# Attention inside a one-core diffusion step: a third bank for scores, the row sums of a tile in one stretch, and GpSimd's second addition without its wait for the split

## What is computed

```
def _block_attention(q, k, v):          # q (B,Lq,H,D), k/v (B,Lk,KVH,D)
    ...
    def one(qblk):                      # blocks of 128 queries
        s = jnp.einsum('bqkgd,bskd->bkgqs', qblk, k).astype(jnp.float32) * scale
        p = jax.nn.softmax(s, axis=-1).astype(v.dtype)
        return jnp.einsum('bkgqs,bskd->bqkgd', p, v)
...
aq = _rmsnorm(aq.reshape(B, L, AT_HEADS, AT_HD), p['q_norm_g'])
keys = jnp.concatenate([_apply_rope(ak, cos, sin), cache['k'].astype(ak.dtype)], axis=1)
vals = jnp.concatenate([av, cache['v'].astype(av.dtype)], axis=1)
y_at = _block_attention(_apply_rope(aq, cos, sin), keys, vals)
```

## Time and profile before

| | |
|---|---|
| median of three runs | 2370.05 us |
| profiled execution, its own time | 2371.3 us |
| its span, first to last instruction | 2369.5 us |
| TensorE matmuls busy in the span | 2280.0 us, 96% |
| VectorE / ScalarE / GpSimd busy | 1390.6 / 805.7 / 336.2 us |
| granted TensorE clock, mean | 0.988 |
| the eight tiles | about 1163.5 to 1391.9 us of the span |

### The profile page before, as it was taken

One profiled execution on the slowest core, in us unless ns is written; L12 is line 12 of the kernel. 1 busy time (PEld: TensorE's weight loads), 2 busy tenths in 40 slices (PEclk: granted clock), 3 DMA queues, 4 the chain that ended last, 5 costly groups with the idle time before them and its releaser, 6 DMA issues. The chain is left out here.

```text
span 2369.5 us, 42943 instructions
## 1 busy us (share of the span) xinstructions
PE 2280.0 (96%) x17607; PEld 2025.9 (85%) x17607; DVE 1390.6 (59%) x2116; ACT 805.7 (34%) x1398; POOL 336.2 (14%) x291
## 2 busy tenths in 40 slices
PE   6999999999999899998899989998999999999997
PEld 5887779999999889998755569877999999998886
DVE  4331266533555466665555446768676676677877
ACT  5321132213333233223344444325323223234444
POOL 0000000001110011111377631000111111120001
PEclk9999999999999999999999989999999999999999
DMA  6325632235452532224101038421222222259434
GB/s 279 121 85 182 225 112 104 104 127 210 155 170 88 199 107 76 89 71 158 44 19 68 36 120 309 153 89 59 79 105 91 79 105 91 74 181 273 130 97 124
DMA packets 126875, 295.55 MB, mean 125 GB/s; under 512 B 19809, under 2 KB 63281, under 8 KB 117377
## 3 DMA queue, kind: packets, MB, share of 16 engines
q1 hardware_dynamic: 98112, 238.67, 29.9%
q10 hardware_dynamic: 24640, 39.46, 4.5%
q0 software_dynamic: 3968, 15.21, 1.7%
HBM read 207.83 MB, written 85.53 MB: 124 GB/s over the span
## 5 line engine op out<-in xcount | busy, mean ns | idle before, releaser
L62 PE MATMUL ps<-prj_w,h_hi 128*128 128x512 f32 (+1 forms) x864 | 255.1, 379 | 4.5 <-DVE h_lo L755 4.5
L62 PE MATMUL ps<-h_hi,fill_whi 128*128 128x384 f32 x672 | 235.4, 350 | 4.9 <-ACT fill_st L1119 2.4
L62 PE MATMUL ps<-h_lo,fill_whi 128*128 128x384 f32 x672 | 226.3, 337 | 3.8 <-issue 3.8
L62 PE MATMUL ps<-wt 128*128 128x320 f32 (+2 forms) x1046 | 227.2, 327 | 2.3 <-DVE merged L3341 1.3
L62 PE MATMUL ps<-h_hi,fill_wlo 128*128 128x384 f32 x672 | 226.4, 337 | 0.2 <-issue 0.2
L62 PE MATMUL ps<-ys,mergedr 128*128 128x256 f32 (+1 forms) x1056 | 219.3, 296 | 0.4 <-issue 0.4
L62 PE MATMUL ps<-zb,mergedr 128*128 128x320 f32 (+2 forms) x764 | 200.4, 327 | 4.9 <-issue 2.7
L62 PE MATMUL ps<-zb,wt 128*128 128x384 f32 (+3 forms) x758 | 200.2, 325 | 0.0
L62 PEld LDWEIGHTS ps<-prj_w,h_hi 128*128 128x128 f32 x864 | 158.1, 191 | 43.1 <-issue 10.6
L62 PEld LDWEIGHTS ps<-wt 128*128 128x128 f32 x1046 | 179.6, 189 | 16.7 <-issue 2.6
L62 PEld LDWEIGHTS ps<-ys,mergedr 128*128 128x128 f32 x1056 | 174.2, 190 | 0.7 <-issue 0.7
(11 more groups left out here) (508 smaller groups left out, 4694.9 us busy)
## 6 DMA issues: line engine op xcount, KB each, us to landing
wraw<-in_w_ffn_in SPq DMA_DIRECT2D x22, 1024.0 KB, 5.2
prj_raw<-in_w_ada SPq DMA_DIRECT2D x16, 1024.0 KB, 5.9
fill_raw<-in_w_fill SPq DMA_DIRECT2D x30, 512.0 KB, 4.6
wtf<-a_dram SPq DMA_DIRECT2D x55, 256.0 KB, 2.6
bg_dram<-fill_st ACTq DMA_DIRECT2D x72, 192.0 KB, 2.0
xf<-bg_dram POOLq DMA_DIRECT2D x24, 576.0 KB, 7.5
tok_dram<-prj_tst ACTq DMA_DIRECT2D x45, 256.0 KB, 2.1
prj_raw<-in_w_tok SPq DMA_DIRECT2D x10, 1024.0 KB, 7.1
```

The costliest lines, as they stand in the source:

```text
L62: mm = pe.matmul(out, lhs[a], rhs[b], start=first and n == 0, stop=last and n == 2, skip_group_check=onto)
```

## The change

- **Third score bank.** `ST` now means banks 4, 5 and 6; score u = 18i + m goes to bank 4 + u mod 3 and waits for the exponential three scores before. The row sums leave bank 6 for bank 3.
- **Row sums in one stretch.** The sums of tile i-1 are computed in tile i, all three trios at once, behind head 2. Trio buffers that hold sums get four slots (two of them over the staging buffers of `branch`); the others stay two and two. `shifts` of the next tile, which uses bank 3 as well, waits for the reciprocal.
- **Score halves between maxima.** The scores are issued by m: 4, 3, 4, 3 and 4 of them between heads, instead of 4, 4, 4, 2 and 4. ScalarE's copies of queries and shifts stand at m = 4 and 11.
- **GpSimd.** The wait of the second additions for the split is removed.
- **Edges.** The query transposes of tile 1 move ahead of the last half product of `branch`. ScalarE makes three of the six copies for the next phase in tile 6 and three in tile 7; VectorE makes the subtractions one by one, the last behind the last normalization.

```diff
-    RING, TRIO = 6, 3
+    TRIO, SLOTS = 3, 4
...
-            pt = [over(f"pt{i}", [P, KV, G * P]) for i in range(RING)]
+            pt = [over(f"pt{i}", [P, KV, G * P]) for i in range(4)]
+            trio = [over(f"trio{i}", [P, KV, G * P]) for i in range(2)]
...
+        def held(n):
+
+            b, r = divmod(n, TRIO)
+            return trio[b % SLOTS] if r == TRIO - 1 else pt[b % 2 * 2 + r]
+
...
                 gp.wait_ge(sem["paired"], 2 * n + 1)
-                if split is not None and split[0] <= LAST:
-                    gp.wait_ge(sem["part"], 2 * split[0] + split[1] + 1)
                 gp.tensor_tensor(c[:], c[:], b[:], ALU.add).then_inc(sem["paired"], 1)
...
             def shifts(i, kv):
                 pe.wait_ge(sem["mx"], AH * i + G * kv + G)
                 pe.wait_ge(sem["pte"], turn(i, 2 + kv))
+                if kv == 0 and i >= 2:
+                    pe.wait_ge(sem["rc"], i - 1)
...
-                if u >= 2:
-                    pe.wait_ge(sem["ex"], u - 1)
+                if u >= 3:
+                    pe.wait_ge(sem["ex"], u - 2)
+                if u == 2:
+                    pe.wait_ge(sem["b0ev"], 24)
...
-                out, at = ps[:, ST + kv, :], slice(j * P, j * P + P)
+                out, at = ps[:, ST + u % 3, :], slice(j * P, j * P + P)
...
+            def sums(i):
+
+                pe.wait_ge(sem["pte"], (turn(i + 2, 1) if i + 2 <= LAST else turn(LAST, 3)) + 1)
+                if i == LAST:
+                    pe.wait_ge(sem["norm"], i)
+                for g in range(NT // TRIO):
+                    n = NT // TRIO * i + g
+                    if n < LASTG:
+                        pe.wait_ge(sem["paired"], 2 * n + 2)
+                        mm = add(held(TRIO * n + TRIO - 1), g == 0, g == 2)
+                    else:
+                        for x in range(TRIO):
+                            mm = add(held(TRIO * n + x), False, x == TRIO - 1)
                 mm.then_inc(sem["sums"], 1)
...
                 shifts(i, 1)
                 head(0)
-                step(0)
-                step(1)
+                steps(0, 4)
                 head(1)
                 if more:
                     queries(i + 1, 1)
-                step(2)
-                step(3)
+                steps(4, 7)
                 head(2)
                 if i:
-                    sums(3 * i - 1)
+                    sums(i - 1)
                 values(i, 0)
                 head(3)
-                step(4)
-                step(5)
+                steps(7, 11)
                 head(4)
                 if more:
                     shifts(i + 1, 0)
-                step(6)
+                steps(11, 14)
                 head(5)
                 if i:
                     spread_sums(i - 1)
                 values(i, 1)
-                sums(3 * i)
                 head(6)
-                step(7)
-                step(8)
+                steps(14, 18)
                 head(7)
                 if i + 2 <= LAST:
                     queries(i + 2, 0)
                 values(i, 2)
-                sums(3 * i + 1)
...
                 shift_scores(0, 2 * u - 39)
+                if u == 23:
+                    queries(1, 0)
                 branch(range(u, u + 1), (2, 4))
-            queries(1, 0)
...
-                for j in range(NT):
-                    exponentials(i, j)
-                    if more and j == 1:
+                for m in range(2 * NT):
+                    if more and m == 4:
                         queries(i + 1, 1)
-                    if more and j == 5:
+                    if more and m == 11:
                         shifts(i + 1, 0)
-                    if not more and j < 6:
-                        ahead(j)
+                    exponentials(i, m // KV, m % KV)
+                    if i >= LAST - 1 and m in (7, 13, 17):
+                        ahead(3 * (i - LAST + 1) + (7, 13, 17).index(m))
...
+                    if i == LAST and h in (0, 1, 2):
+                        ahead(h)
                     if i >= 1 and h == 2:
                         inverted(i - 1)
-                    if i == LAST and h == 5:
-                        ahead()
+                    if i == LAST and h == 3:
+                        ahead(3)
...
+            ahead(4)
             inverted(LAST)
             normed(LAST)
+            ahead(5)
```

More of the change, by code:

```diff
@@ L1925, in attention @@
         STAGES = 6
+        with ExitStack() as later:
+            trio += [later.enter_context(nc.sbuf_tensor(f"att_trio{i}", [P, KV, G * P], F32)) for i in range(2, SLOTS)]
         b0st = [ph.sb(f"b0st{i}", [P, TH]) for i in range(STAGES)]
@@ L1930, in attention @@
         block = ph.block()
-        PT, ST, SB, OB = 3, 4, 6, 7
+        PT, ST, OB = 3, 4, 7
+        def held(n):
+            b, r = divmod(n, TRIO)
+            return trio[b % SLOTS] if r == TRIO - 1 else pt[b % 2 * 2 + r]
         SHIFTS = range(0, 3)
@@ L2027, in rope, with add_trio @@
                 gp.wait_ge(sem["rope"], 6 * n + 3 * e + 3)
-            def add_trio(n, split=None):
-                a, b, c = (pt[(TRIO * n + x) % RING] for x in range(TRIO))
+            def add_trio(n):
+                a, b, c = (held(TRIO * n + x) for x in range(TRIO))
                 gp.wait_ge(sem["pv"], n + 1)
@@ L2046, in _ @@
                 if i:
-                    add_trio(3 * i - 1, (i + 1, 1))
+                    add_trio(3 * i - 1)
                 if i + 2 <= LAST:
@@ L2052, in _ @@
                     rope(i + 2, 1)
-                add_trio(3 * i + 1, (i + 2, 0))
+                add_trio(3 * i + 1)
                 if i + 3 <= LAST:
@@ L2188, in values @@
                     for kv in range(KV):
-                        mm = pe.matmul(ps[kv * HD:kv * HD + HD, OB, :], va[:, j, kv, 0:HD], pt[n % RING][:, kv, :],
+                        mm = pe.matmul(ps[kv * HD:kv * HD + HD, OB, :], va[:, j, kv, 0:HD], held(n)[:, kv, :],
                                        start=j == 0, stop=j == NT - 1)
@@ L2195, in add @@
                     for a in range(G):
-                        mm = pe.matmul(ps[32 * a:32 * a + 32, SB, kv * P:kv * P + P], ones[:], x[:, kv, a * P:a * P + P],
+                        mm = pe.matmul(ps[32 * a:32 * a + 32, PT, kv * P:kv * P + P], ones[:], x[:, kv, a * P:a * P + P],
                                        start=first and kv == 0, stop=last and kv == KV - 1)
                 return mm
[L2200 to L2210, removed]
+            def sums(i):
[10 more added lines that the diff above has]
+                            mm = add(held(TRIO * n + x), False, x == TRIO - 1)
                 mm.then_inc(sem["sums"], 1)
@@ L2215, in spread_sums @@
                 pe.wait_ge(sem["rc"], i + 1)
[L2216 to L2219, removed]
+                if i < LAST - 1:
+                    pe.wait_ge(sem["pte"], turn(i + 2, 2) + 1)
                 for a in range(G):
@@ L2228, in tile, with steps @@
                 more = i < LAST
-                def step(j):
-                    for kv in range(KV):
-                        scores(i, kv, j)
+                def steps(first, last):
+                    for m in range(first, last):
+                        scores(i, m % KV, m // KV)
                 def head(h):
@@ L2287, in _ @@
                 shift_scores(0, 2 * u - 39)
+                if u == 23:
+                    queries(1, 0)
                 branch(range(u, u + 1), (2, 4))
-            queries(1, 0)
             for i in range(LAST + 1):
                 tile(i)
-            sums(LASTG)
+            sums(LAST)
             pe.wait_ge(sem["b1lo"], 5)
@@ L2356, in shifts, with exponentials @@
                 act.activation(qm[i % 2][kv][0:H1, :], ps[0:H1, PT, :], ACT.Copy).then_inc(sem["pte"], 1)
-            def exponentials(i, j):
+            def exponentials(i, j, kv):
                 n = NT * i + j
[L2360 to L2367, removed]
+                if kv == 0:
+                    b, r = divmod(n, TRIO)
+                    if b >= 2 and r < 2:
+                        act.wait_ge(sem["paired"], 2 * b + r - 3)
+                    if b >= SLOTS and r == 2:
+                        act.wait_ge(sem["sums"], (b - SLOTS) // TRIO + 1)
+                    if b == 2 and r == 2:
+                        for s in range(STAGES):
+                            act.wait_ge(sem[f"b0out{s}"], 16 * 24 // STAGES)
+                u = 2 * n + kv
+                act.wait_ge(sem["s2"], u + 1)
+                act.activation(held(n)[:, kv, :], ps[:, ST + u % 3, :], ACT.Exp, scale=QS).then_inc(sem["ex"], 1)
             def output(i):
@@ L2408, in _ @@
             shifts(0, 0)
+            queries(1, 0)
             store(range(23, 24))
             put(23)
-            queries(1, 0)
             for i in range(LAST + 1):
                 tile(i)
-            for i in range(STAGES):
-                act.wait_ge(sem[f"b0out{i}"], 16 * 24 // STAGES)
         @block.vector
@@ L2523, in inverted @@
```

(11 more changed lines are left out.)

## The result

The changed kernel takes 2382.62 us (median of five runs, 2377.8 to 2389.97), the kernel before 2370.05 (now the median of five as well): a ratio of 1.006, 95% interval 1.0037 to 1.0082. It is slower, by 12.6 us. The profiled execution is the longest of the five, 2389.97 us.

A forecast was written before the change was run, and what follows sets the result against it. TensorE was taken to set the attention loop's pace. Gains of 27.1 us, against 26.1 of stalls from the removed hold and 8 of lost clock, gave +7 us: 2377 us against the median, range 2341 to 2391.

The forecast's parts named there:

- the mechanism: Attention tiles: TensorE's query transposes wait for splits late behind GpSimd's unheld additions; 2377 us, 2365 to 2391, chance 0.56.
- Rival A: Both split places: the subtraction escapes GpSimd's second addition, TensorE never waits; 2343 us, 2338 to 2350, chance 0.22.
- B: Only the second place, the second half of tile i+1's split, stalls; 2358 us, 2352 to 2365, chance 0.14.
- The hold: Splits behind unheld additions: first half 2.25 us (first place), second half 1.9 us, six tiles each; 26.1 us with restarts.
- The clock: TensorE after the pauses: lower clock, 1.7 us lost behind 4 or 5 of twelve, 8 us; bounds 0 and 20.
- Third bank: Score matmuls in seven tiles: four waits for exponentials a tile vanish, 0.52 us each, 2.1 us a tile.
- The margin of 0.08 us: Fourth score with three banks: the first exponential ends at 1.33 us, the score wants to start at 1.41.
- Halves: Scores as 4, 3, 4, 3, 4 between maxima: the next head's wait for VectorE's maximum goes, 0.45 us a tile.
- Sums: Row sums, 48 matmuls in one stretch: 1.4 us instead of 1.71, 0.3 us less in six tiles.
- Start: Tile 1's query transposes ahead of the last half of the branch product: 1.24 us wait goes, 1.2 us gained.
- Last tile: Last tile, three of six copies moved a tile earlier: 32.1 us becomes 25.5, gain 6.6, between 3 and 8.
- Last subtraction: Next-phase subtraction behind the last normalization, beside the last output transfer: a loss of 0.4 us.

The follow-up runs named there:

- experiments 1 to 5: Holds of second additions back (both, first half, second half); kernel before without hold; changed kernel, short second addition: 2344.46, 2364.52, 2360.34, 2386.70, 2344.47 us.
- experiment 3: The changed kernel with only the second addition of trio 3i-1 held, for the second half of tile i+1's split: 2360.34 us, ratio 0.9959.
- experiment 4: The kernel before with its hold removed and nothing else changed: 2386.70 us, ratio 1.0069.
- experiment 5: The changed kernel, no hold, with the second addition on 128 of 1024 columns only: 2344.47 us, ratio 0.9903.
- experiments 8 to 10: Changed kernel with splits moved and a first addition held; then query normalization first; then tile 0 as with both holds: 2350.83, 2348.17, 2344.17 us.
- experiment 1: The changed kernel with both of GpSimd's second additions held for the split again: 2344.46 us; run twice more as controls, 2347.03 and 2346.39 us.
- experiment 6: The changed kernel with both second additions held and two score banks instead of three: 2365.40 us, ratio 0.9985.
- experiment 7: The changed kernel with both second additions held and the old 4, 4, 4, 2 and 4 scores between heads: 2346.78 us, ratio 0.9914.
- experiment 9: The changed kernel with splits moved, a first addition held, and the first half of the query normalization put first at head 5: 2348.17 us, ratio 0.9910.
- the two places alone: The changed kernel with only the first half's or only the second half's second addition held: 2364.52 and 2360.34 us.

## Why the prediction was right, point by point

**What was expected and where it landed.** 2377 us, slower, by GpSimd's unheld additions; measured 2382.6 us. The way was a near thing in the forecast, 0.41 for slower against 0.39 for faster; the mechanism was given 0.56, and it is what the traces show. Rival A (the split escapes) falls with experiments 1 to 5, B (only the second place) with the pauses of 2.15 us in the first place and with experiment 3. Two parts of the sum came out otherwise than reasoned, the clock and the last tile.

**The hold.** Twelve pauses were expected, six of 2.25 us and six of 1.9. Measured: six of 1.77, five of 2.16 and, in tile 0, one of 1.06 us (where head 7 had already waited 1.2 us for its maximum), 22.5 us against 24.9. The cast's blocking, which no row of before showed, is seen in the trace after (0.67 us and up to 1.37 us in place of 0.28) and most plainly in experiment 4 (2.10 us). The rule of the Trainium skill (SBUF — State Buffer, "Who interferes with whom") that a cast can enter a mode that shares both ports, and that whoever issues first keeps them for the whole instruction, agrees with these rows and with experiment 5, where a shorter addition makes the delay shorter; the mode itself no trace shows. The prediction took it as blocked because it moves as many words a ns as a two-input operation does; no run tests that reason, and an operation with one input of 8 elements (experiments 8 to 10) was blocked as well.

**The clock** is the term that was mis-sized, and it stands on both sides of the sum. 8 us of loss were expected, 1.7 us behind four or five pauses of twelve. The profiled execution lost 16 to 17 in tiles 1 to 6, as much as behind ten of them, but it is the longest of the five, and the kernel before lost 5 us in its last tile that the changed one does not lose. Over the whole program the profiled executions have mean clocks of 0.983 and, before, 0.988: 41 against 28 us of work, 12 more. The median run has 0.985: 36 us, 7 more. Each 0.001 is some 2.4 us of work, so the rounding alone leaves this open by about 2. The clock also makes most of the spread: the five runs go from 2377.8 us at 0.987 to 2389.97 at 0.983. Against the profiled runs with both held (0.991 and 0.992) the median run's 0.985 accounts for 14 to 16 us of the 36 to 38 between them, not all of it inside the tiles, and the pauses for the rest. How much of the clock in a median run is due to the pauses alone was not isolated.

**The gains.** 27.1 us expected, 22 to 26 measured (experiment 1 and its controls). *Third bank:* 2.1 us a tile expected in seven tiles, 14.7 us; experiment 6 gives 1.95 a middle tile, and 4.5 more in the last one, where the prediction gave the bank nothing. The margin of 0.08 us was just about used up: from the first matmul of a stretch's fourth score to its second it is up to 0.31 us in place of 0.24 (1248.83 to 1249.14 in the changed kernel), which costs less than 0.1 us each time. *Halves:* 0.45 us a tile expected; the traces of experiment 7 show 0.48, 3.4 us in seven tiles; by its time it stays open. *Sums:* 48 matmuls in 1.45 us (1233.50 to the next start at 1234.95), 1.4 expected. *Start:* 1.24 us of waiting are gone: from head 7 to the next transposes 1160.96 to 1163.23, 2.3 us, where 1159.96 to 1163.49 took 3.5. *Last tile:* expected 25.5 us; it starts at 1382.04, and the product behind it starts at 1407.50, 25.46. The number is right, but the reason only in small part, so that is luck: of the 6.7 us gained some 5 are the clock, which read 0.84 there before (0.16 x 32 us) and reads 1.00 now, and the prediction did not read it. It put the gain down to the copies that were moved; with the same copies moved but two score banks (experiment 6) the last tile still takes 29.94 us at a clock of 0.87, so the copies and the rest of the order give some 2 us and the third bank 4.5. *Last subtraction:* 0.4 us given for it; TensorE's pause to the next phase is 2.20 us against 2.21, so it costs nothing. What is missing of the gains in the tiles is the cast that GpSimd still blocks in the held kernel, 0.55 us in six tiles: experiment 9 takes these out (25.67 us a tile).

## What to carry to other kernels

- An operation that another engine waits for should start where the engine it shares memory ports with has nothing under way. A wait on the idle engine in front of its long instruction can be worth far more than it costs: here 10.5 us of waiting on GpSimd buy 36 us.
- Before a wait is taken out, lay the two engines' instructions side by side in the new order, to a tenth of a microsecond, with the call times and not only the durations. Any edit in front (here 0.57 us of sums taken away, or a split put ahead) moves the meeting, and the next operation to suffer may be the smallest one.
- A pause on TensorE is not only its own length: count the clock behind it. Here pauses of 1.8 to 2.2 us went with some 0.9 to 1.4 us of lost work each, and pauses of 1.05 and 1.24 us (experiment 4) with almost none. Whether they cost more the closer they stand is not shown: the two places alone lost 5 and 7 us, both together 16 to 17, but in the longest of five executions.
- Read the clock of the kernel before in every stretch whose length goes into the sum, the last tile too: a gain there can be clock that comes back.

## What the runs showed of the hardware that was not expected

- An operation of VectorE on 128x8 elements, 0.17 us alone, takes up to 2.30 us behind one of GpSimd's additions: being small did not spare it. VectorE's maxima, which read PSUM, stayed at 1.34 to 1.36 us in the same traces, under the additions as well (1247.62 in the changed kernel).
- Called in the same hundredth of a microsecond (1248.99, experiment 4), the cast went first, and GpSimd's addition was 0.14 us longer for it.
